# Layer 2's attention: the softmax division moved from the probabilities to a turned row that multiplies a head pair's outputs

## The chip, the core and the metric

The kernel runs as one program on one core of a Trainium2 chip. The metric is the device time of one execution in microseconds (us); the time before is the median of three runs. TensorE (PE in the profile) multiplies matrices, VectorE is DVE, ScalarE is ACT, GpSimd is POOL, SyncE (SP) issues most DMA transfers. Each engine takes its instructions in the order in which the program gives them and waits at semaphores for the others. TensorE writes PSUM banks; GpSimd works on SBUF.

## The reference, cut to what matters

Two layers over a sequence of 512 tokens and a width of 1024, batch 1, float32. The change lies in layer 2, which has two attentions over the same normed input: eight heads of a dilated window attention, and eight heads of a latent (low rank) attention.

```python
h = rmsnorm(x, norm_gain)
proj = jnp.matmul(h, w_in)
q_a, k_a, v_a, z_a, c_q, c_kv, k_rope, z_b = jnp.split(proj, idx, axis=-1)
...
# per head and block of 128 queries, in both attentions:
s = einsum(q, k) * scale + bias            # masked above the diagonal
p = exp(s - m)                             # m: row maximum
o = einsum(p, v) / sum(p)                  # the division this change moves
...
mixed = jnp.concatenate([o_a * jax.nn.silu(z_a), o_b * jax.nn.silu(z_b)], axis=-1)
out = x + jnp.matmul(mixed, w_out)
```

## The kernel before

All projections of both layers form a list of groups (`GROUPS`); a group is a product of 512 tokens by up to 512 columns, taken in up to 8 slabs of 128 rows of the weights, and a slab in four quarters `t`. Values are kept as a high and a low part, so a quarter is three matmuls of 512 columns (L1637 to L1639, tiles `w_hi`, `w_lo` with `hT_hi`, `hT_lo` or `cT_hi`, `cT_lo`). ACT makes `w_hi` of a slab (L564), POOL makes `w_lo` (L893), three slabs ahead of PE.

Layer 2's attentions have 16 heads in 8 pairs `p`: pairs 0 to 3 are of the dilated, 4 to 7 of the latent attention. A pair has four query blocks `i`, so there are `N` = 32 steps `n = 4p + i`, each with two heads `j`, and rows of 128(i+1) keys. The steps have no time of their own: a generator `heads()` on each engine is cut into three parts for each step (called a, b and c here), and `heads_due(v)` says how many parts are done by the time of projection quarter `v`, counted from the start of the group `G_VALUES`. On PE the parts stand between the projection matmuls of `G_VALUES`, the two `G_UKV` groups, `G_GATES` and the one after it, and the first half of `G_OUT2`, which is the first of the two groups of the final projection. On the other engines the same parts stand between the casts of weights, evacuations and the norms of the latent attention (`latent_norms`, rows L1100 to L1117 and L1548 to L1556 on DVE; `latent_queries` on POOL, L957 and L961).

What a step does before the change:

1. PE: scores of both heads into banks `A[0]` and `A[1]` (L1843).
2. DVE: adds bias or mask, writes the negated scores into `probs` (tile `sgd_sb`) and their minimum into `nmax` (L1424).
3. ACT: `exps`, exponential in place with the row sum in `rsum` (L758).
4. DVE: reciprocal of the two sums into `rinv` (L1443).
5. POOL: `scale`, probabilities by reciprocal and by 0.5 (L1001), once for each head.
6. PE: `turn_probs`, transposes of the 128x128 blocks into the one bank `A[2]` (L1852), which waits for the scaling, and for DVE to have emptied `A[2]`.
7. DVE: `turned_probs`, copies them out to `turned_place` (L1433, tiles `pT` or `sgd_sb`).
8. PE, once for each pair: `outputs`, values by turned probabilities (L1866) into `A[3]`, which then holds the pair's outputs with heads and features on the partitions and the 512 queries on the columns. The trace counts 40 matmul records for them.
9. ACT: `pair_raw` copies `A[3]` to `o_raw(p)` (L746). POOL: `gate` multiplies by the gate (L1008). ACT: `split` makes the high part (L753). POOL: `low` makes the low part (L1016), which is the stationary or moving operand of slab `p` of the final projection.

`heads_turn` (L1826) transposes queries and keys of the coming pair, into `A[2]` too (the second of all into `A[3]`), and ACT empties it (L738). The first two of them stand at slab 4 of `G_VALUES`. They wait for the norms of the keys on DVE (L1177).

`heads_due` before: the first part at quarter 20, 9 parts by quarter 32, then one a quarter, and two a quarter from quarter 120; 106 parts in all.

Of the kernel before, what the change touches and what calls it, by code (L numbers as in the profile page):

```python
# [20 lines left out]
ALU = mybir.AluOpType  # L21
# [104 lines left out]
HEAD_STEPS = 3 * (4 * H + 3) + 1  # L126
HEADS_FIRST, HEADS_SECOND, HEADS_THIRD = 20, 33, 120
# [6 lines left out]
def heads_due(v):  # L134

    if v < HEADS_FIRST:
        return 0
    if v < HEADS_SECOND:
        return 9 * (v - HEADS_FIRST + 1) // (HEADS_SECOND - HEADS_FIRST)
    if v < HEADS_THIRD:  # L140
        return 9 + (v - HEADS_SECOND + 1)
    return min(HEAD_STEPS, 9 + HEADS_THIRD - HEADS_SECOND + 2 * (v - HEADS_THIRD + 1))

# [41 lines left out]
GATE_STEP = {19: 0, 20: 1, 21: 2, 22: 3, 29: 4, 30: 5, 31: 6, 35: 7}  # L185
SPLIT_STEP = {20: 0, 21: 1, 22: 2, 28: 3, 30: 4, 31: 5, 32: 6, 35: 7}
# [45 lines left out]
def build(nc, a):  # L232
    with ExitStack() as ctx:
# [89 lines left out]
        h_inv, h_scaled, h_pt, h_pt_out, h_o = sem("h_inv"), sem("h_scaled"), sem("h_pt"), sem("h_pt_out"), sem("h_o")  # L323
# [144 lines left out]
        def _(sp):  # L468
# [82 lines left out]
        def _(act):  # L551
# [188 lines left out]
            def heads():  # L740
# [3 lines left out]
                def pair_raw(p):  # L744
                    act.wait_ge(h_o, p + 1 if p < H - 1 else H + 1)
                    act.copy(o_raw(p), A[3][:, :]).then_inc(pair_out, 1)  # L746

                def split(n):
                    if n in SPLIT_STEP:
                        p = SPLIT_STEP[n]  # L750
                        act.wait_ge(pair_gated, p + 1)
                        act.wait_ge(z_ready, 4 * G_GATES if p < 3 else 4 * G_OUT2)
                        act.copy(pair_split(p)[0], o_raw(p)).then_inc(pair_hi, 1)  # L753
# [7 lines left out]
                for n in range(N + 3):  # L761
                    if n >= 7 and n % 4 == 3:
                        pair_raw(n // 4 - 1)
                    if n < N:
                        exps(n, 0)
                        exps(n, 1)
                    yield
                    if turn_at(n):
                        heads_turned(*turn_at(n))
                    yield  # L770
                    split(n)
                    yield
                pair_raw(H - 1)
                split(N + 3)
# [103 lines left out]
        def _(pool):  # L878
# [113 lines left out]
            def heads():  # L992
# [17 lines left out]

                def low(n):
# [6 lines left out]
                for n in range(N + 3):  # L1018
                    low(n - 1)
                    if 1 <= n < N + 1:  # L1020
                        scale(n - 1, 0)
                    yield
                    if 1 <= n < N + 1:
                        scale(n - 1, 1)
                    yield
                    gate(n)
                    yield
                gate(N + 3)
                low(N + 3)
# [54 lines left out]
        def _(dve):  # L1084
# [322 lines left out]
            def heads():  # L1407
# [27 lines left out]

                scores(0, 0)
                scores(0, 1)
                for n in range(N + 3):
                    if 0 <= n - 2 < N:
                        turned_probs(n - 2, 0)  # L1440
                    if 1 <= n < N + 1:
                        dve.wait_ge(h_exp, 2 * n)
                        dve.reciprocal(rinv[:, n - 1, 0:2], rsum[:, n - 1, 0:2]).then_inc(h_inv, 1)  # L1443
                    yield
                    yield
                    if 0 <= n - 2 < N:
                        turned_probs(n - 2, 1)
                    if n + 1 < N:
                        scores(n + 1, 0)
                        scores(n + 1, 1)  # L1450
                    yield
                yield
# [179 lines left out]
        def _(pe):  # L1632
# [197 lines left out]
            def heads():  # L1830
# [24 lines left out]

                def outputs(p, blocks):

                    pe.wait_ge(h_pt_out, 2 * (4 * p + blocks[-1]) + 2)
                    if p == 0:
                        pe.wait_ge(z_by_act, act_evacs[G_VALUES + 1])  # L1860
                    elif blocks[0] == 0:
                        pe.wait_ge(pair_out, p)
# [8 lines left out]
                for n in range(N + 3):  # L1871
                    if 0 <= n - 2 < N:
                        turn_probs(n - 2, 0)
# [12 lines left out]
                    if 0 <= n - 2 < N:  # L1886
                        turn_probs(n - 2, 1)
                    p, c = divmod(n - 6, 4)
                    if c == 0 and 0 <= p < H - 1:
                        outputs(p, range(4))  # L1890
                    if n == N + 1:
                        outputs(H - 1, range(3))
                    if n == N + 2:
# [20 lines left out]
            def project(g):  # L1914
# [22 lines left out]
                for k in range(0 if g else 1, nk):  # L1937
# [13 lines left out]
                    if k == 4 and g == G_VALUES:  # L1951
# [99 lines left out]
```

## Time and profile before

| what | value |
|---|---|
| time, median of 3 runs | 940.93 us (940.06 to 941.17) |
| profiled execution, its own time | 940.87 us |
| its span | 939.1 us |
| PE busy | 915.1 us, 97% |
| POOL busy | 473.7 us, 50% |
| ACT busy | 396.1 us, 42% |
| DVE busy | 394.2 us, 42% |
| granted clock of PE, mean | 0.998 |

The attention steps of layer 2 lie between about 737 and 906 us of the span. In a timeline a row gives the start, the time from the first start to the last end, and the instructions merged in it; ends of matmuls are modelled, so on PE the distance between two starts tells more than the length of a row. A wait in square brackets is idle time ahead of a row and the instruction that ended it.

### The profile page before, as it was taken

The page shows a single profiled execution, that of the slowest core. Times are in us where ns is not written, and L with a number is a line of the kernel's source. Part 1 is how long each engine was busy: PE and PEld are TensorE (multiplying, and loading weights), DVE is VectorE, ACT ScalarE, POOL GpSimd, SP SyncE. Part 2 cuts the span into 40 slices and gives each one's busy share as a digit, 9 for nine tenths or more (in the row PEclk, how much of TensorE's full clock was granted, in tenths as well). Part 3 has the DMA queues.
Part 4 walks back from the last instruction along what each step waited for, and adds up shares of the span by engine and source line. Part 5 has one row for each costly group of instructions (what it writes and reads, how often), then busy time and mean ns, then how long its engine had stood idle before and what let it go on. Part 6 is the DMA issues. An engine that isn't in the chain of part 4 may idle for free. (4 is left out here: it accounts for less than half of the span.)

```text
span 939.1 us, 12624 instructions
## 1 busy us (share of the span) xinstructions
PE 915.1 (97%) x4640; PEld 725.3 (77%) x4640; DVE 394.2 (42%) x951; ACT 396.1 (42%) x873; POOL 473.7 (50%) x440
## 2 busy tenths in 40 slices
PE   9999999999999999999999999999999988999988
PEld 7877888887888877777777788788888655677767
DVE  4310139044114413567474434415429756544521
ACT  4533442334223344454554432325535663555521
POOL 5543436434546654655444334553447494465662
PEclk9999999999999999999999999999999999999999
DMA  8422211322322322122112242332523221111113
GB/s 306 147 91 76 82 45 46 112 68 89 112 90 90 106 87 77 49 87 68 55 58 68 63 162 68 108 101 77 151 68 107 68 90 46 33 36 46 46 46 112
DMA packets 41709, 80.77 MB, mean 86 GB/s; under 512 B 3328, under 2 KB 5120, under 8 KB 41648
## 3 DMA queue, kind: packets, MB, share of 16 engines
q1 hardware_dynamic: 41504, 79.95, 27.2%
q8 instruction: 37, 0.61, 0.3%
q14 instruction: 24, 0.20, 0.1%
q10 hardware_dynamic: 144, 0.02, 0.0%
HBM read 77.84 MB, written 2.12 MB: 85 GB/s over the span
## 5 line engine op out<-in xcount | busy, mean ns | idle before, releaser
L893 POOL TENSOR_TENSOR w_lo<-raw,w_hi 128x512 fp32r<-128x512 f32 (+1 forms) x262 | 343.5, 1319 | 387.0 <-ACT w_hi L564 385.9
L1637 PE MATMUL Z<-w_hi,hT_hi 128*128 128x512 f32 (+1 forms) x804 | 324.2, 403 | 4.0 <-POOL w_lo L893 2.7
L1639 PE MATMUL Z<-w_hi,hT_lo 128*128 128x512 f32 (+1 forms) x804 | 313.1, 389 | 0.0
L1638 PE MATMUL Z<-w_lo,hT_hi 128*128 128x512 f32 (+1 forms) x804 | 312.3, 388 | 0.0
L564 ACT CAST w_hi<-raw 128x512 fp32r<-128x512 f32 (+1 forms) x262 | 157.3, 614 | 247.8 <-PE Z L1639 224.0
L1637 PEld LDWEIGHTS Z<-w_hi,hT_hi 128*128 128x128 f32 x804 | 151.1, 188 | 45.8 <-issue 12.9
L1639 PEld LDWEIGHTS Z<-w_hi,hT_lo 128*128 128x128 f32 x804 | 150.9, 188 | 31.5
L1638 PEld LDWEIGHTS Z<-w_lo,hT_hi 128*128 128x128 f32 x804 | 151.4, 188 | 26.8 <-issue 0.2
L1001 POOL TENSOR_SCALAR sgd_sb<-sgd_sb,rinv 128x128 f32<-128x128 f32 (+3 forms) x64 | 37.1, 587 | 42.9 <-DVE rinv L1443 42.1
L1637 PE MATMUL Z<-w_hi,oT_hi 128*128 128x512 f32 x128 | 51.1, 399 | 0.5 <-DVE prob L1209 0.5
L1358 DVE CUSTOM_DVE_ANT_0 x_sb<-A,bias 128x128 f32<-128x128 f32 (+3 forms) x64 | 28.6, 484 | 53.8 <-PE A L1766 53.8
L717 ACT ACTIVATE x_sb<-x_sb,nmax 128x128 f32<-128x128 f32 (+3 forms) x64 | 35.4, 555 | 36.4 <-DVE nmax L1358 36.4
L1639 PE MATMUL Z<-w_hi,oT_lo 128*128 128x512 f32 x128 | 50.0, 391 | 0.0
L1638 PE MATMUL Z<-w_lo,oT_hi 128*128 128x512 f32 x128 | 49.9, 390 | 0.0
L758 ACT ACTIVATE sgd_sb<-sgd_sb,nmax 128x128 f32<-128x128 f32 (+3 forms) x64 | 35.5, 556 | 30.1 <-DVE nmax L1424 30.1
L1433 DVE COPY pT<-A 128x384 f32<-128x384 f32 (+2 forms) x40 | 22.3, 556 | 42.3 <-PE A L1852 39.9
L1852 PE MATMUL A<-ident,sgd_sb 128*128 128x128 f32 x160 | 29.9, 286 | 8.4 <-POOL sgd_sb L1001 4.0
L1852 PEld LDWEIGHTS A<-ident,sgd_sb 128*128 128x128 f32 x160 | 19.2, 142 | 23.6 <-DVE pT L1433 8.2
L1843 PE MATMUL A<-kT,qT 64*128 64x128 f32 (+7 forms) x128 | 34.2, 454 | 0.1
L1235 DVE TENSOR_TENSOR x_sb<-x_sb,Z 128x512 f32<-128x512 f32 x16 | 10.9, 688 | 52.8 <-PE Z L1639 52.8
L1637 PE MATMUL Z<-hT_hi,w_hi 128*128 128x512 f32 x64 | 32.3, 505 | 0.0
L580 ACT ACTIVATE z_sb<-Z,rms 128x512 f32<-128x512 f32 (+1 forms) x40 | 26.2, 682 | 12.7 <-PE Z L1639 12.5
(220 smaller groups left out, 1204.1 us busy)
## 6 DMA issues: line engine op xcount, KB each, us to landing
raw<-in_w_in SPq DMA_DIRECT2D x91, 512.0 KB, 3.6
raw<-in_w_out SPq DMA_DIRECT2D x16, 512.0 KB, 3.4
x_sb<-in_x SPq DMA_DIRECT2D x8, 512.0 KB, 5.6
raw<-in_ret_w_o SPq DMA_DIRECT2D x8, 512.0 KB, 3.3
raw<-in_diff_w_o SPq DMA_DIRECT2D x8, 512.0 KB, 3.4
out<-x_sb SPq DMA_DIRECT2D x8, 256.0 KB, 2.8
raw<-in_w_in SPq DMA_DIRECT2D x4, 416.0 KB, 3.2
sgd_sb<-in_xT SPq DMA_DIRECT2D x3, 512.0 KB, 7.1
```

The costliest lines, as they stand in the source:

```text
L564: act.copy(w_hi[:, s % SPLIT_SLOTS, 0:width], raw[:, c % RAW_SLOTS, s - CHUNK_START[c], 0:width]).then_inc(hi_ready, 1)
L580: act.activation((z_ret if g < G_RET else z_sb)[:, t, arg:arg + width], Z[t][:, 0:width], ACT.Copy, scale=rms[:, layer, 0, t:t + 1]).then_ ...
L717: act.activation(p, p, ACT.Exp, bias=nmax[:, j, n:n + 1], scale=-1.0, accum_out=rsum[:, n, j:j + 1]).then_inc(s_exp, 1)
L758: act.activation(probs[:, n % 4, j, 0:w], probs[:, n % 4, j, 0:w], ACT.Exp, bias=nmax[:, j, n:n + 1], scale=-1.0, accum_out=rsum[:, n, j:j ...
L893: pool.tensor_tensor(w_lo[:, s % SPLIT_SLOTS, 0:width], raw[:, c % RAW_SLOTS, s - CHUNK_START[c], 0:width], w_hi[:, s % SPLIT_SLOTS, 0:wid ...
L1001: pool.tensor_scalar(p, p, rinv[:, n, j:j + 1], 0.5, ALU.mult, ALU.mult).then_inc(h_scaled, 1)
L1358: dve.tensor_tensor_reduce(diff_probs(j, n, w), A[j][:, score_columns(i, True)], bias[:, h % 2, S - w:S], -1.0, TOP, ALU.add, ALU.min, nma ...
L1637: pe.matmul(out, l_hi, r_hi, start=first, stop=False)
L1638: pe.matmul(out, l_hi, r_lo, start=False, stop=False)
L1639: return pe.matmul(out, l_lo, r_hi, start=False, stop=last)
L1843: pe.matmul(A[j][:, score_columns(i, shared)], qT[rows, slot, P * i:P * (i + 1)], kT[rows, slot, 0:P * (i + 1)], start=True, stop=True).th ...
L1852: last = pe.transpose(A[2][:, kk], probs[:, m % 4, j, kk], ident[:, :])
```

## The change

What it does:

- `scale` on POOL is gone. `turn_probs` waits for the exponentials, and transposes unscaled probabilities.
- The reciprocals of a pair (8 columns) are taken by one DVE instruction at the pair's last step, in place of four of 2 columns.
- `pair_spread` (ACT) spreads them over 512 columns into `o_raw(p)`. `turn_row` (PE) transposes the four 128x128 blocks of this into `row_bank(p)`, which is `A[3]` (for the last pair `A[0]`). `pair_row` (ACT) copies the bank back to `o_raw(p)`.
- `outputs` waits for that copy, since it writes the same bank. `pair_end` (DVE) then multiplies the bank, 0.5 and the row. It stands in the place of ACT's `pair_raw`. For the last pair POOL multiplies the row by the gate beforehand (`row_gated`), and ACT's high part follows `pair_end` at once.
- The parts of a step stand in another order, and the first pair's `heads_turn` stands one slab later (slab 5). `heads_due` starts at quarter 23 with one part a quarter to the end; 103 parts in all. The bias of pair 2 is loaded two slabs earlier in SP's queue.

```diff
-HEAD_STEPS = 3 * (4 * H + 3) + 1
-HEADS_FIRST, HEADS_SECOND, HEADS_THIRD = 20, 33, 120
+HEAD_STEPS = 3 * (4 * H + 2) + 1
+HEADS_FIRST = 23
...
-    return min(HEAD_STEPS, 9 + HEADS_THIRD - HEADS_SECOND + 2 * (v - HEADS_THIRD + 1))
+    return max(0, min(HEAD_STEPS, v - HEADS_FIRST + 1))
...
+        def row_bank(p):
+            return A[3] if p < H - 1 else A[0]
...
-                for p, at in enumerate(((G_LAYER2 + 1, 0), (G_LAYER2 + 1, 0), (G_GATES, 6), (G_GATES + 1, 0))):
+                for p, at in enumerate(((G_LAYER2 + 1, 0), (G_LAYER2 + 1, 0), (G_GATES, 4), (G_GATES + 1, 0))):
...  ACT
-                def pair_raw(p):
-                    act.wait_ge(h_o, p + 1 if p < H - 1 else H + 1)
-                    act.copy(o_raw(p), A[3][:, :]).then_inc(pair_out, 1)
+                def pair_spread(p):
+                    act.wait_ge(h_inv, p + 1)
+                    r = rinv[:, 4 * p:4 * p + 4, :].rearrange("p i j -> p (i j)").unsqueeze(2).broadcast_to([P, 8, 64])
+                    act.copy(o_raw(p).rearrange("p (n e) -> p n e", e=64), r).then_inc(row_spread, 1)
+
+                def pair_row(p):
+                    act.wait_ge(row_turned, p + 1)
+                    act.copy(o_raw(p), row_bank(p)[:, :]).then_inc(row_evicted, 1)
...
-                if g == G_VALUES and k == 4:
+                if g == G_VALUES and k == 5:
                     heads_turned(0, 0)
                     heads_turned(0, 1)
...  POOL
-                def scale(n, j):
-                    w = P * (n % 4 + 1)
-                    if j == 0:
-                        pool.wait_ge(h_inv, n + 1)
-                    p = probs[:, n % 4, j, 0:w]
-                    pool.tensor_scalar(p, p, rinv[:, n, j:j + 1], 0.5, ALU.mult, ALU.mult).then_inc(h_scaled, 1)
...
+                def row_gated(p):
+                    pool.wait_ge(row_evicted, p + 1)
+                    pool.wait_ge(th_used, 8 + p + 1)
+                    pool.tensor_tensor(o_raw(p), o_raw(p), gateT[:, p, :], ALU.mult).then_inc(pair_first, 1)
...  DVE
+                def pair_end(p):
+                    if p == H - 1:
+                        dve.wait_ge(pair_first, 1)
+                    dve.wait_ge(h_o, p + 1 if p < H - 1 else H + 1)
+                    dve.scalar_tensor_tensor(o_raw(p), A[3][:, :], 0.5, o_raw(p), ALU.mult, ALU.mult).then_inc(pair_out, 1)
...
+                    if n < N and n % 4 == 3:
+                        dve.wait_ge(h_exp, 2 * n + 2)
+                        dve.reciprocal(rinv[:, n - 3:n + 1, :], rsum[:, n - 3:n + 1, :]).then_inc(h_inv, 1)
...  PE
-                    pe.wait_ge(h_scaled, 2 * m + j + 1)
+                    pe.wait_ge(h_exp, 2 * m + j + 1)
...
+                def turn_row(p):
+                    pe.wait_ge(row_spread, p + 1)
+                    if p == H - 1:
+                        pe.wait_ge(h_max, 8 * H)
+                    elif p:
+                        pe.wait_ge(pair_out, p)
+                    for i in range(4):
+                        cc = slice(P * i, P * (i + 1))
+                        last = pe.transpose(row_bank(p)[:, cc], o_raw(p)[:, cc], ident[:, :])
+                    last.then_inc(row_turned, 1)
```

Where the instructions stand now. First PE, between the last two pairs, in the order before. The projection matmuls between the rows are left out; L1852 turns probabilities, L1843 are scores, L1866 a pair's outputs.

```order
L1852 MATMUL A<-ident,sgd_sb 128x128 [waits h_scaled,h_pt_out]
L1852 MATMUL A<-ident,sgd_sb 128x128 x3
...
L1843 MATMUL A<-kT,qT 128x384 [waits h_max] x2
...
L1852 MATMUL A<-ident,sgd_sb 128x128 [waits h_scaled,h_pt_out]
L1852 MATMUL A<-ident,sgd_sb 128x128 x3
...
L1852 MATMUL A<-ident,sgd_sb 128x128 [waits h_scaled,h_pt_out]
...
L1843 MATMUL A<-kT,qT 128x512 [waits h_max] x2
...
L1852 MATMUL A<-ident,sgd_sb 128x128 [waits h_scaled,h_pt_out]
L1866 MATMUL A<-sgd_sb,m_sb 64x128 [waits pair_out,h_pt_out]
```

The same place on PE now, where L1865 turns probabilities, L1879 turns the row, L1856 are scores and L1894 the outputs.

```order
L1865 MATMUL A<-ident,sgd_sb 128x128 [waits h_exp,h_pt_out]
L1865 MATMUL A<-ident,sgd_sb 128x128 x3
L1879 MATMUL A<-ident,z_sb 128x128 [waits pair_out,row_spread]
L1879 MATMUL A<-ident,z_sb 128x128 x3
...
L1865 MATMUL A<-ident,sgd_sb 128x128 [waits h_exp,h_pt_out]
L1865 MATMUL A<-ident,sgd_sb 128x128 x3
...
L1856 MATMUL A<-kT,qT 128x384 [waits h_max] x2
...
L1894 MATMUL A<-sgd_sb,m_sb 64x128 [waits row_evicted,h_pt_out]
L1894 MATMUL A<-sgd_sb,m_sb 64x128 x5
L1894 MATMUL A<-pT,m_sb 64x128 x14
L1865 MATMUL A<-ident,sgd_sb 128x128 [waits h_exp,h_pt_out]
```

The outputs moved ahead of the next pair's first turn and of the widest scores, and the row's turn stands behind the first four-block turn; the wait for scaling became one for exponentials.

Second, PE at the end of the attention, before: the two four-block turns and the last pair's outputs, with hardly a projection between.

```order
L1852 MATMUL A<-ident,sgd_sb 128x128 [waits h_scaled,h_pt_out]
L1852 MATMUL A<-ident,sgd_sb 128x128 x2
L1852 MATMUL A<-ident,sgd_sb 128x128 [waits h_scaled,h_pt_out]
L1852 MATMUL A<-ident,sgd_sb 128x128 x3
...
L1852 MATMUL A<-ident,sgd_sb 128x128 [waits h_scaled,h_pt_out]
L1852 MATMUL A<-ident,sgd_sb 128x128 x3
L1866 MATMUL A<-pT,m_sb 64x128 [waits pair_out,h_pt_out]
```

And the same place now.

```order
L1865 MATMUL A<-ident,sgd_sb 128x128 [waits h_exp,h_pt_out]
L1865 MATMUL A<-ident,sgd_sb 128x128 x3
L1879 MATMUL A<-ident,z_sb 128x128 [waits h_max,row_spread]
L1879 MATMUL A<-ident,z_sb 128x128 x3
L1894 MATMUL A<-pT,m_sb 64x128 [waits pair_out,h_pt_out]
L1894 MATMUL A<-pT,m_sb 64x128
L1894 MATMUL A<-sgd_sb,m_sb 64x128 x4
L1894 MATMUL A<-pT,m_sb 64x128 x6
...
L1865 MATMUL A<-ident,sgd_sb 128x128 [waits h_exp,h_pt_out]
L1865 MATMUL A<-ident,sgd_sb 128x128 x3
```

Three of four output blocks moved ahead of the last turn, and none of the rows waits for scaling.

Third, DVE between the last two pairs. L1433 before and L1436 now empty the turned probabilities, L1424 and L1427 write the masked scores, L1443 is before the reciprocal and now `pair_end`. Before:

```order
L1433 COPY pT<-A2 128x128 [waits h_o,h_pt]
L1443 RECIPROCAL rinv<-rsum 128x2 [waits h_exp]
L1433 COPY pT<-A2 128x128 [waits h_o,h_pt]
L1424 ISA sgd_sb,nmax<-A0,dist 128x512 [waits h_mm,h_pt]
L1424 ISA nmax 128x1
L1424 ISA sgd_sb,nmax<-A1,dist 128x512 [waits h_mm,h_pt]
L1424 ISA nmax 128x1
L1433 COPY sgd_sb<-A2 128x256 [waits h_o,h_pt]
L1443 RECIPROCAL rinv<-rsum 128x2 [waits h_exp]
```

Now:

```order
L1436 COPY pT<-A2 128x128 [waits h_o,h_pt]
L1443 SCALAR_TENSOR_TENSOR z_sb<-A3,z_sb 128x512 [waits h_o]
L1427 ISA sgd_sb,nmax<-A0,dist 128x512 [waits h_mm,h_pt]
L1427 ISA nmax 128x1
L1436 COPY sgd_sb<-A2 128x256 [waits h_o,h_pt]
L1427 ISA sgd_sb,nmax<-A1,dist 128x512 [waits h_mm,h_pt]
L1427 ISA nmax 128x1
L1436 COPY sgd_sb<-A2 128x256 [waits h_o,h_pt]
```

The two scores of a step no longer stand side by side ahead of a copy, the reciprocals with their wait for the exponentials are gone from three steps in four, and a 512 column product is new.

## Rows read from the trace of the kernel before

**Rows 1.** Page, part 1: busy time, share of the span, instructions.
```profile
PE 915.1 (97%) x4640; PEld 725.3 (77%) x4640; DVE 394.2 (42%) x951; ACT 396.1 (42%) x873; POOL 473.7 (50%) x440
```

**Rows 2.** Windows: length, busy time by engine, PE clock, DMA share and rate.
```profile
800.00:840.00 40.00, 39.54 (x259) 28.08 (x257) 19.78 (x64) 21.40 (x53) 19.71 (x25) 1.00 0.14 41
...
900.00:902.00 2.00, 2.00 (x11) 1.40 (x12) 0.79 (x2) 0.00 (x0) 0.62 (x1) 0.50 0.04 9
```

**Rows 3.** Waits of PE, 720 to 939 us: total us, times, longest.
```profile
PE A L1852 <- POOL sgd_sb L1001: 4.0, 2, 2.4
PE A L1852 <- DVE sgd_sb L1433: 2.2, 1, 2.2
PE A L1826 <- DVE z_sb L1177: 1.4, 1, 1.4
PE A L1826 <- DVE sgd_sb L1433: 1.2, 2, 0.7
PE A L1852 <- DVE pT L1433: 1.2, 1, 1.2
PE A L1826 <- DVE pT L1433: 0.7, 1, 0.7
```

**Rows 4.** Timeline of PE, a quiet stretch of pairs 6 and 7.
```profile
883.52 0.39 PE L1638 MATMUL Z<-w_lo,cT_hi 128*128 128x512 f32 x1
883.75 0.40 PE L1639 MATMUL Z<-w_hi,cT_lo 128*128 128x512 f32 x1
883.99 0.60 PE L1852 MATMUL A<-ident,sgd_sb 128*128 128x128 f32 x4
884.34 0.47 PE L1637 MATMUL Z<-w_hi,cT_hi 128*128 128x512 f32 x1
...
884.88 0.40 PE L1639 MATMUL Z<-w_hi,cT_lo 128*128 128x512 f32 x1
885.37 0.33 PE L1852 MATMUL A<-ident,sgd_sb 128*128 128x128 f32 x1
...
888.61 0.39 PE L1639 MATMUL Z<-w_hi,hT_lo 128*128 128x512 f32 x1
888.84 0.27 PE L1852 MATMUL A<-ident,sgd_sb 128*128 128x128 f32 x1
889.05 0.88 PE L1866 MATMUL A<-sgd_sb,m_sb 128*64 128x128 f32 x12
889.75 1.70 PE L1866 MATMUL A<-pT,m_sb 128*64 128x128 f32 x28
891.38 0.50 PE L1637 MATMUL Z<-w_hi,hT_hi 128*128 128x512 f32 x1
```

**Rows 5.** Timeline of PE, end of the attention.
```profile
895.54 0.40 PE L1639 MATMUL Z<-w_hi,hT_lo 128*128 128x512 f32 x1
895.89 0.55 PE L1852 MATMUL A<-ident,sgd_sb 128*128 128x128 f32 x3
898.86 0.63 PE L1852 MATMUL A<-ident,sgd_sb 128*128 128x128 f32 x4 [2.42 <-POOL sgd_sb L1001]
...
900.27 1.12 PE L1852 MATMUL A<-ident,sgd_sb 128*128 128x128 f32 x4
...
906.35 0.50 PE L1637 MATMUL Z<-w_hi,hT_hi 128*128 128x512 f32 x1
```

**Rows 6.** Timeline of POOL and ACT, end of the attention.
```profile
898.02 1.36 POOL L1001 TENSOR_SCALAR sgd_sb<-sgd_sb,rinv 128x512 f32<-128x512 f32 x2
...
906.46 0.58 ACT L746 COPY z_sb<-A 128x512 f32<-128x512 f32 x1 [1.06 <-PE A L1866]
```

**Rows 7.** Timelines of DVE and of POOL around 773 us.
```profile
773.27 0.18 DVE L1100 TENSOR_SCALAR rs_b<-rs_a 128x32 int32<-128x32 int32 x1
...
773.97 1.23 DVE L1103 TENSOR_TENSOR rs_b<-rstd 128x32 f32<-128x32 f32 x1
...
773.87 1.29 POOL L961 TENSOR_TENSOR z_sb<-z_sb,o_sb 128x512 f32<-128x512 f32 x1
```

More of the change, by code:

```diff
@@ L322, in build @@
         h_turned, h_qk, h_mm, h_max, h_exp = sem("h_turned"), sem("h_qk"), sem("h_mm"), sem("h_max"), sem("h_exp")
-        h_inv, h_scaled, h_pt, h_pt_out, h_o = sem("h_inv"), sem("h_scaled"), sem("h_pt"), sem("h_pt_out"), sem("h_o")
+        h_inv, h_pt, h_pt_out, h_o = sem("h_inv"), sem("h_pt"), sem("h_pt_out"), sem("h_o")
+        row_spread, row_turned, row_evicted, pair_first = (sem(n) for n in ("row_spread", "row_turned", "row_evicted", "pair_first"))
         w_first, x_hi, x_lo = sem("w_first"), sem("x_hi"), sem("x_lo")
@@ L759, in exps @@
                                    scale=-1.0, accum_out=rsum[:, n, j:j + 1]).then_inc(h_exp, 1)
-                for n in range(N + 3):
-                    if n >= 7 and n % 4 == 3:
-                        pair_raw(n // 4 - 1)
+                for n in range(N + 2):
+                    if n >= 5 and n % 4 == 1 and n < N:
+                        pair_row(n // 4 - 1)
                     if n < N:
@@ L766, in heads @@
                         exps(n, 1)
+                    if n >= 4 and n % 4 == 0:
+                        pair_spread(n // 4 - 1)
                     yield
@@ L770, in heads @@
                     yield
+                    if n == N:
+                        pair_row(H - 1)
                     split(n)
                     yield
-                pair_raw(H - 1)
-                split(N + 3)
+                split(N + 2)
                 yield
@@ L1016, in low @@
                         pool.tensor_tensor(lo_, o_raw(p), hi_, ALU.subtract).then_inc(pair_lo, 1)
-                for n in range(N + 3):
+                for n in range(N + 2):
                     low(n - 1)
-                    if 1 <= n < N + 1:
-                        scale(n - 1, 0)
+                    if n == N + 1:
+                        row_gated(H - 1)
                     yield
-                    if 1 <= n < N + 1:
-                        scale(n - 1, 1)
                     yield
@@ L1027, in heads @@
                     yield
-                gate(N + 3)
-                low(N + 3)
+                low(N + 2)
                 yield
@@ L1434, in turned_probs @@
                                     A[2][:, 0:P * (i + 1)].rearrange("p (b s) -> p b s", s=P)).then_inc(h_pt_out, 1)
+                def pair_end(p):
[3 more added lines that the diff above has]
+                    dve.scalar_tensor_tensor(o_raw(p), A[3][:, :], 0.5, o_raw(p), ALU.mult, ALU.mult).then_inc(pair_out, 1)
                 scores(0, 0)
                 scores(0, 1)
[L1438 to L1445, printed above, removed]
+                for n in range(N + 2):
                     if 0 <= n - 2 < N:
                         turned_probs(n - 2, 1)
+                    if n >= 6 and n % 4 == 2 and n < N:
+                        pair_end((n - 6) // 4)
+                    yield
                     if n + 1 < N:
                         scores(n + 1, 0)
+                    yield
+                    if 1 <= n < N + 1:
+                        turned_probs(n - 1, 0)
+                    if n + 1 < N:
                         scores(n + 1, 1)
+                    if n < N and n % 4 == 3:
+                        dve.wait_ge(h_exp, 2 * n + 2)
+                        dve.reciprocal(rinv[:, n - 3:n + 1, :], rsum[:, n - 3:n + 1, :]).then_inc(h_inv, 1)
                     yield
+                pair_end(H - 1)
                 yield
@@ L1860, in outputs @@
                         pe.wait_ge(z_by_act, act_evacs[G_VALUES + 1])
+                    if p < H - 1:
+                        pe.wait_ge(row_evicted, p + 1)
                     elif blocks[0] == 0:
@@ L1870, in heads @@
                 scores(0, (0, 1))
-                for n in range(N + 3):
+                for n in range(N + 2):
                     if 0 <= n - 2 < N:
-                        turn_probs(n - 2, 0)
+                        turn_probs(n - 2, 1)
                     yield
@@ L1885, in heads @@
                     yield
-                    if 0 <= n - 2 < N:
-                        turn_probs(n - 2, 1)
-                    p, c = divmod(n - 6, 4)
+                    p, c = divmod(n - 5, 4)
                     if c == 0 and 0 <= p < H - 1:
                         outputs(p, range(4))
+                    if 1 <= n < N + 1:
+                        turn_probs(n - 1, 0)
+                    if n >= 4 and n % 4 == 0:
+                        turn_row(n // 4 - 1)
+                    if n == N:
+                        outputs(H - 1, range(3))
                     if n == N + 1:
-                        outputs(H - 1, range(3))
-                    if n == N + 2:
                         outputs(H - 1, (3,))
```

17 lines of the change are left out of this document (7 added, 10 removed).

## The prediction

> **What bounds the kernel now.** I read the page's busy shares first: PE is busy 97% of the span and no other engine over 50% [rows 1]. So the time is PE's own work plus PE's idle time, and anything on another engine counts only where PE waits for it. Then the windows: in 800 to 840 us, in the middle of layer 2's attention, PE is busy 39.54 of 40 us at a granted clock of 1.00, its level of 2.4 GHz [rows 2]. There the change can win nearly nothing and can only add PE work. Then PE's waits from 720 us on, which is where the change lies [rows 3]. They are 10.7 us in all, and every one ends at a transposition. They have three kinds: waits for POOL's scaling (two, together 4.0 us, the longest 2.4 at the end of the attention [rows 5]), one of 1.4 us for the norms of the keys ahead of the very first turn, and five for DVE to have emptied bank A[2] (2.2 + 1.2 + 1.2 + 0.7, together 5.3 us). Last the timeline, since ends of matmuls are modelled and distances between starts are safer. Projection matmuls follow each other at 0.23 us (883.52 to 883.75) [rows 4], so whatever a distance has over that is the work or the wait between.
>
> **The change, part by part.** The sum is made against the profiled execution's own 940.87 us (span 939.1, the rest around it), which is 0.06 under the median of 940.93.
>
> *The turned row, added PE work.* Eight pairs get four transpositions each, L1879. Four of the same shape cost 884.34 - 883.75 - 0.23 = 0.36 us between two projection matmuls, and the next matmul starts some 0.08 late as well: 0.44 us [rows 4]. Lower bound 0.36, since in front of them stand other transpositions for all pairs, so no change of kind is paid twice; upper bound the whole merged row, 0.60. I take 0.44, eight times: **+3.5 us** (2.9 to 4.8). None of it can be hidden on a full PE.
>
> A page speaks against this price. The Trainium skill, "TensorE: Matmul & The Clock Gate", Part 4 (PE-mode transpose), gives about 275 ns for a 128x128 transposition in a kernel's context. A lone one here does read 0.27 us (at 888.84) [rows 4], so the trace agrees for one by itself, but four of them need 0.44 together. By the page's figure taken 32 times the term would be an estimated 8.8 us in place of 3.5; by the rows it is 3.5.
>
> *Scaling leaves POOL.* 64 instructions go. What that gives PE is the two waits, of which 1.6 us lie near 759 us and the 2.4 us belong to the end, below: **-1.6 us**. What comes next there is the exponential on ACT, which stands five or six parts ahead of the turn, so nearly five quarters of about 0.69 us (three matmuls), more than an exponential's row with its hops; I book nothing for it.
>
> *The end of the attention.* From the projection matmul at 895.54 to that at 906.35 there are 10.81 us [rows 5]. In it lie ten starts of projection matmuls, 2.3 us. The other 8.5 us are a three-block and two four-block turns and the last pair's 40 output matmuls. At quiet prices: a pair's outputs and one transposition take 891.38 - 888.61 - 0.23 = 2.54 us [rows 4], two gaps of four 0.88, one of three some 0.35, and 0.1 for splitting the outputs: 3.9 us. So 4.6 us are wait, and its echo. PE stood 2.42 us for POOL, whose scaling began only at 898.02 [rows 6], behind other work in its queue. After that the granted clock was 0.50 in 900 to 902, which is the level of 1.2 GHz [rows 2], and the four-block turn took 1.12 us against 0.63 at 898.86 [rows 5]. In the new order nothing in this stretch waits for POOL, one part stands in each quarter, the exponentials of the last step are some five parts old, and three of four output blocks need only turns that lie behind. **-4.6 us** (2.4 if the slow clock and the short waits came all the same). Behind it the chain to the last slab shrinks: `pair_end` on DVE (bounded by ACT's copy of this size, 0.58 [rows 6], and twice that), the high part, the low part, against eight quarters or 5.5 us of projections. It lies hidden. It would cost if POOL were over 2 us late there.
>
> *The first turn, one slab later.* Four quarters, 2.8 us, stand ahead of it now, and the wait was 1.4: **-1.4 us**, with what is late next (DVE's norms) below.
>
> *The five waits for A[2].* Here the order on DVE decides. Before, both scores of a step stood together between two copies; now there is one score between copies. Reciprocals with their wait for ACT fall from 32 to 8. Against that `pair_end` is new, 8 times some 0.6 to 0.7 us, in a part with one copy. The largest waits are in 765 to 790 us, where DVE also has the latent norms to do, and these run slow: a 128x32 instruction takes 1.23 us at 773.97 while one of the same width took 0.18 just before, and it ends when a POOL instruction ends that began at 773.87 and took 1.29 [rows 7]. The POOL work that stays (rotations and low parts) still does that, but the scaling no longer does, and no longer delays the rotations. I take half of the 5.3 us: **-2.6 us** (0 to -5.3). The value is in the middle since rows speak for both.
>
> The page "SBUF — State Buffer" of the Trainium skill, section "SBUF: two separate sides", says that VectorE and GpSimd share one port pair as an exclusive lock, held for a whole instruction. The trace agrees [rows 7]. By that rule less POOL work is worth more than its own waits.
>
> *Short waits of the old order.* The one-block turn behind a four-block turn waits for the copy: 885.37 - 884.88 - 0.23 = 0.26 us [rows 4], in seven pairs, 1.8 us. In the new order the row's turn or the outputs stand between. Three four-block turns behind a `heads_turn` of the first pairs wait about as much. Of 2.6 us I take **-2.2** (0 to -2.6).
>
> *New waits.* `turn_row` waits for `pair_spread`: one ACT instruction of 512 columns (0.58 by the nearest row [rows 6]) behind two exponentials and a reciprocal. From the turn that releases the last DVE score to the row's turn PE has three quarters, 2.1 us, and two turns, 0.8; the chain needs some 2.3. `outputs` waits for `pair_row`, again 0.58, across two quarters. ACT gains 8 copies of 0.58, in the first pairs where it is nearly full. I book **+0.6** (0 to 3; behind the waiting PE all projections queue). Other edits (the bias load two slabs earlier in SP's queue, which waits for scores that are long done) cost nothing; if the load held up a weight transfer, it has 12 quarters of cover.
>
> Sum: 3.5 - 1.6 - 4.6 - 1.4 - 2.6 - 2.2 + 0.6 = -8.3 us. 940.87 - 8.3 = **932.6 us**.
>
> **The rivals.**
> *DVE bounds the first half.* PE gets to the early turns sooner, but the norms on DVE end no sooner, and the waits that are removed there come back as waits for A[2]. Then 1.6, 1.4 and 2.6 fall out: -8.3 + 5.6 = -2.7, **938.2 us**. For it: the waits for A[2] are already the larger part and rows 7 show DVE held up by POOL work that stays. Against it: after these 50 us DVE has room.
> *DVE is freed wholly.* The other 2.7 of the 5.3 go too and there is no new wait: **929.3 us**.
> *Transpositions don't overlap.* If each of the 32 new ones cost its own 0.27 us, as the single one does [rows 4], they are 8.6 us, 5.1 more than booked: **937.7 us**. The four-block rows speak against it. The page on TensorE named above would have it so.
> *The row comes late (slower).* In each pair reciprocal, spread, turn, copy and outputs form a chain across ACT. If the spread with its repeated elements is slow, or ACT is behind, PE stands in part c of each pair with all projections behind it. The slack is about 0.5 us; with 8.3 us gained elsewhere it decides from 1.0 us of wait a pair. A spread of four times 0.58 us would be 1.7 late, 1.2 of wait; with ACT's later work pushed back, and a clock that falls as at 900 us, I take 1.5 a pair: 12 us, less the 0.6 booked: **944 us**. For it speaks only that the operation isn't in the trace.
>
> **How the numbers follow.** Forecast 0.60, DVE bound 0.15, DVE freed 0.13, no overlap 0.04, late row 0.08. A measurement of this kernel can tell about 0.2%, 1.9 us, from no change. The first four cases are faster by more than that, though the DVE bound case with a row some 0.2 us late a pair is within: faster 0.88, same 0.05, slower 0.07. The range takes in the freed case and its best prices at the lower end (929.3 less some of the 0.6 that the row's lower bound gives), and most of the DVE bound case at the upper: 928.5 to 937.5. Left out are the late row and what of the second case lies above.
>
> **What would show it.** In the changed kernel's profile: no POOL instruction on `sgd_sb` in the attention; at its end the four-block turns without an idle time ahead, and a clock of 1.00 there; the row's turns with a distance of 0.4 to 0.5 us over the projections and little idle ahead; ACT's spread at about 0.6 us; PE's waits for copies from A[2] down to about 3 us, all before 790 us. PE busy time should be up by some 2 to 3 us where the records count the new turns. The forecast is wrong if PE waits for `row_spread` or `row_evicted` in every pair, if the early waits come back whole, or if the clock falls at some new place.

## The result and the profile after

The changed kernel takes 930.32 us (median of 4 runs, 929.72 to 930.96) against 940.92 us for the kernel before (4 runs, 940.06 to 941.17). The ratio is 0.9889, with a 95% interval from 0.9872 to 0.9906: 10.6 us or 1.1% faster. The profiled execution took 930.71 us, its span is 928.9 us against 939.1. One later execution of the changed kernel ran at a granted clock of 0.75 and took 1134.08 us; it is left out where its repeat is compared below.

The page, part 1, of the changed kernel (busy time, share of the span, instructions) answers to [rows 1]:

```profile
PE 913.7 (98%) x4672; PEld 728.1 (78%) x4672; DVE 396.3 (43%) x935; ACT 400.6 (43%) x881; POOL 438.3 (47%) x376
```

The 32 new transpositions are there (4672 against 4640) and POOL lost 64 instructions and 35 us. PE is still the bound. Its busy time did not rise. Ends of matmuls are modelled longer than their distance, so that waits up to some 0.15 us (a row reads 0.39 us where the next starts after 0.23) count as busy, and so do slow matmuls at half the clock; both became fewer. A busy sum is no price for an added instruction here, the distances between starts are.

The waits of PE from 715 us on (total us, times, longest), against [rows 3]:

```profile
PE A L1865 <- DVE pT L1436: 1.6, 2, 0.8
PE A L1839 <- DVE sgd_sb L1436: 1.1, 1, 1.1
PE Z L1650 <- POOL w_lo L901: 0.2, 1, 0.2
PE A L1839 <- DVE pT L1436: 0.2, 1, 0.2
```

No wait for scaling is left, none for the norms of the keys ahead of the first turn, and none for `row_spread` or `row_evicted`. The waits for DVE to empty `A[2]` fell from 5.3 to 2.9 us.

The end of the attention on PE (start, time, instructions), against [rows 5]:

```profile
887.84 0.40 PE L1652 MATMUL Z<-w_hi,hT_lo 128*128 128x512 f32 x1
888.19 0.55 PE L1865 MATMUL A<-ident,sgd_sb 128*128 128x128 f32 x3
...
889.97 0.60 PE L1865 MATMUL A<-ident,sgd_sb 128*128 128x128 f32 x4
890.40 0.60 PE L1879 MATMUL A<-ident,z_sb 128*128 128x128 f32 x4
890.93 0.44 PE L1894 MATMUL A<-pT,m_sb 128*64 128x128 f32 x4
...
893.21 0.60 PE L1865 MATMUL A<-ident,sgd_sb 128*128 128x128 f32 x4
...
895.13 1.09 PE L1894 MATMUL A<-pT,m_sb 128*64 128x128 f32 x16
896.15 0.50 PE L1650 MATMUL Z<-w_hi,hT_hi 128*128 128x512 f32 x1
```

From 887.84 to 896.15 there are 8.31 us with 16 projection starts of 0.2275 (four took 0.91 us from 729.62 to 730.53 in the kernel before), so 4.7 us are left for the same turns and outputs and the row's turn. Before, it was 8.5 us without the row. The clock stayed up, as the windows show (length, busy by engine, clock, DMA share, GB/s), where [rows 2] had 0.50:

```profile
888.00:892.00 4.00, 4.00 (x39) 3.33 (x39) 1.49 (x4) 2.10 (x4) 3.70 (x3) 1.00 0.02 4
892.00:896.00 4.00, 4.00 (x39) 3.08 (x34) 0.69 (x1) 0.76 (x2) 3.24 (x3) 1.00 0.42 131
```

The price of the row, in a quiet pair of the changed kernel:

```profile
813.90 0.40 PE L1652 MATMUL Z<-hT_hi,w_lo 128*128 128x512 f32 x1
814.13 0.60 PE L1865 MATMUL A<-ident,sgd_sb 128*128 128x128 f32 x4
814.57 0.60 PE L1879 MATMUL A<-ident,z_sb 128*128 128x128 f32 x4
814.92 0.47 PE L1650 MATMUL Z<-hT_hi,w_hi 128*128 128x512 f32 x1
```

Eight transpositions take 814.92 - 813.90 - 0.23 = 0.79 us, four took 0.36 in [rows 4]: the row costs 0.43 us a pair. Yet a quiet pair did not get longer. From one pair's outputs to the next the kernel before takes 870.94 - 850.98 = 19.96 us, the changed one 859.09 - 839.22 = 19.87:

```profile
850.98 0.88 PE L1866 MATMUL A<-sgd_sb,m_sb 128*64 128x128 f32 x12
...
870.94 0.44 PE L1866 MATMUL A<-pT,m_sb 128*64 128x128 f32 x4
```

```profile
839.22 0.88 PE L1894 MATMUL A<-sgd_sb,m_sb 128*64 128x128 f32 x12
...
859.09 0.44 PE L1894 MATMUL A<-pT,m_sb 128*64 128x128 f32 x4
```

The first fence is of the kernel before, the second of the changed one. So some 0.5 us of short waits went in each such pair, of which most are too short to be listed as waits. The largest of them is the second one-block turn: it stood 0.26 us late in [rows 4], and now PE starts it at once:

```profile
842.19 0.40 PE L1652 MATMUL Z<-hT_hi,w_lo 128*128 128x512 f32 x1
842.42 0.27 PE L1865 MATMUL A<-ident,sgd_sb 128*128 128x128 f32 x1
842.45 0.48 PE L1650 MATMUL Z<-hT_hi,w_hi 128*128 128x512 f32 x1
```

Over the projections it costs 842.45 - 842.19 - 0.23 = 0.03 us, where the same turn cost 0.33 before (at 866.83).

What the new instructions of the other engines cost (ACT and DVE groups from 740 us on: count, busy us, mean ns, idle before and releaser):

```profile
L744 ACT COPY z_sb<-rinv 128x512 f32<-128x512 f32 x5 | 3.0, 605 | 1.0 <-DVE rinv L1462 1.0
L748 ACT COPY z_sb<-A 128x512 f32<-128x512 f32 x5 | 2.9, 587 | 5.7 <-PE A L1879 5.7
L1443 DVE SCALAR_TENSOR_TENSOR z_sb<-A,z_sb 128x512 f32<-128x512 f32 x5 | 3.4, 683 | 1.8 <-PE A L1894 1.8
```

Reading one element 64 times costs ACT hardly more than the copy of the row out of PSUM: 605 ns against 587. `pair_end` took 683 ns, in the 0.6 to 0.7 us that the prediction gave it.

### The profile page after: what moved, and what is told of

It reads as the page before. It is cut to its first block, busy times and chain, and to the rows that moved or that the text cites. A ratio compares the mean times of both kernels' runs of the same rounds, so it can differ in the third digit from the quotient of the medians.

```text
span 928.9 us, 12622 instructions
## 1 busy us (share of the span) xinstructions
PE 913.7 (98%) x4672; PEld 728.1 (78%) x4672; DVE 396.3 (43%) x935; ACT 400.6 (43%) x881; POOL 438.3 (47%) x376
## 4 chain that ended last, share of the span: by engine, by line
PE 88%; DVE 5%; POOL 2%; issue 2%; ACT 1%; DMA 1%; SPq 0%; ACTq 0%; DVEq 0%; POOLq 0%
PE Z L1650 24%; PE Z L1652 23%; PE Z L1651 23%; PE A L1856 3%; PE A L1779 2%; PE A L1894 2%; PE A L1865 2%; PE A L1791 2%; PE A L1660 2%; POOL w_lo L901 1%; PE A L1839 1%; PE A L1804 1%; PE Z L1737 1%; PE A L1690 1%; PE A L1764 1%
## 5 line engine op out<-in xcount | busy, mean ns | idle before, releaser
L1436 DVE COPY pT<-A 128x384 f32<-128x384 f32 (+2 forms) x40 | 22.3, 557 | 34.6 <-PE A L1865 34.4
L1856 PE MATMUL A<-kT,qT 64*128 64x128 f32 (+7 forms) x128 | 33.8, 451 | 0.0
L1865 PEld LDWEIGHTS A<-ident,sgd_sb 128*128 128x128 f32 x160 | 19.1, 140 | 16.0 <-DVE pT L1436 5.9
L1865 PE MATMUL A<-ident,sgd_sb 128*128 128x128 f32 x160 | 29.5, 282 | 2.0 <-DVE pT L1436 1.6
L1162 DVE TENSOR_REDUCE stat<-bias 128x4 f32<-128x512 f32 (+1 forms) x16 | 10.7, 683 | 42.8 <-POOL bias L913 42.8
```

Of the source, the lines that this page charges most:

```text
L1436: dve.tensor_copy(turned_place(m, j), A[2][:, 0:P * (i + 1)].rearrange("p (b s) -> p b s", s=P)).then_inc(h_pt_out, 1)
L1856: pe.matmul(A[j][:, score_columns(i, shared)], qT[rows, slot, P * i:P * (i + 1)], kT[rows, slot, 0:P * (i + 1)], start=True, stop=True).th ...
L1865: last = pe.transpose(A[2][:, kk], probs[:, m % 4, j, kk], ident[:, :])
```

## The experiments

My theory was that of the prediction: PE gained the waits, POOL's share of them through the dependency, the others through the order on DVE, and paid 0.43 us a pair. The rivals were that the order alone, or the algebra alone, or POOL's mere occupancy made the gain.

**The algebra alone**, in the old order of steps, with the old end (two parts a quarter) and the first turn at slab 4. Cut from the difference to the kernel before:

```diff
-                    pe.wait_ge(h_scaled, 2 * m + j + 1)
+                    pe.wait_ge(h_exp, 2 * m + j + 1)
...  PE, part a, behind turn_probs(n - 2, 0)
+                    if n >= 5 and n % 4 == 1:
+                        turn_row(n // 4 - 1)
```

> The turned row in the old order of steps: turns wait for exponentials, the row's turn stands behind the first four-block turn's partner, outputs where they were, two parts a quarter at the end, first turn at slab 4. Theory A: before's 940.9 + 3.4 for the row's turns - 1.7 for the scaling wait near 759 us - 3.7 for the wait and the slow clock at the end = 938.9 us (937.5 to 940). Rival (the order brings nothing): 930 to 932 us. Other rival (the algebra brings nothing): 944 us.

Measured: 936.68 us (median of 7 runs), ratio 0.9961 (0.9949 to 0.9974), beside 940.6 us for the kernel before. A little better than my 938.9, under its lower bound: the waits for `A[2]` fell as well, from 5.3 to 3.3 us, with no change on DVE but the missing reciprocals and `pair_end`.

```profile
PE A L1869 <- DVE pT L1441: 1.7, 3, 0.7
PE A L1843 <- DVE z_sb L1185: 1.4, 1, 1.4
PE A L1843 <- DVE sgd_sb L1441: 0.9, 2, 0.7
PE A L1843 <- DVE pT L1441: 0.7, 1, 0.7
```

These are PE's waits in it. Those for scaling are gone, also at the old, packed end. From the projection start at 894.26 to the one at 902.03, with ten projection starts, 5.5 us are left for the same turns and outputs, the row's turn among them, where it was 8.5.

**The order alone**, with scaling on POOL kept and no row; the first turn one slab later and one part a quarter at the end belong to it. Cut from the difference to the changed kernel:

```diff
-                    pe.wait_ge(h_exp, 2 * m + j + 1)
+                    pe.wait_ge(h_scaled, 2 * m + j + 1)
...
-                    if n >= 4 and n % 4 == 0:
-                        turn_row(n // 4 - 1)
...  ACT, part a
+                    if n >= 6 and n % 4 == 2 and n < N:
+                        pair_raw((n - 6) // 4)
```

> The new order of steps alone: probabilities are scaled on GpSimd as before, no turned row, ScalarE copies the outputs, one reciprocal a step. Theory A (the wait for GpSimd was a cause of its own): the row's 3.4 us are saved, but waits for the scaling return, 1.6 us or more around 755 us and 2 to 4 us at the end: 931 to 934 us. Rival (the order is all of the gain): 930.3 - 3.4 = 926.9 us, and no wait for GpSimd above 0.5 us.

Measured: 938.07 us (7 runs), ratio 0.9973 (0.9959 to 0.9986). Slower than either forecast, though it has no row to turn. PE's waits:

```profile
PE A L1849 <- POOL sgd_sb L1005: 5.5, 6, 1.7
PE A L1849 <- DVE pT L1429: 2.6, 4, 0.9
PE A L1823 <- DVE sgd_sb L1429: 1.1, 1, 1.1
```

The new order takes up the turn of head 0 one part earlier. With scaling in the chain that makes PE wait for POOL six times in place of two: 4.7 of the 5.5 us are four waits between 752 and 781 us. At the end it is otherwise:

```profile
894.48 0.40 PE L1636 MATMUL Z<-w_hi,hT_lo 128*128 128x512 f32 x1
895.47 0.52 PE L1849 MATMUL A<-ident,sgd_sb 128*128 128x128 f32 x3 [0.59 <-POOL sgd_sb L1005]
...
903.50 0.50 PE L1634 MATMUL Z<-w_hi,hT_hi 128*128 128x512 f32 x1
```

In these 9.02 us lie 16 projection starts, so 5.4 us are left for the turns and outputs, and the clock is 1.00 in 892 to 904 us. So either half alone takes some 3 of the 3.9 us that the end gained (8.54 to 4.67). The sum comes out otherwise because of the early pairs: alone the two halves bring 2.5 and 3.9 us, together 10.3 (against 940.6), that is 3.8 us more than their sum.

**POOL kept busy.** The changed kernel, with POOL doing 64 multiplications of the old sizes (for the last pair one block less in the widest) at the old places on dead columns, for which no other engine waits:

```diff
+                    if 1 <= n < N + 1:
+                        idle_scale(n - 1, 0)
...
+                    pool.tensor_scalar(spare, dead, cols[:, 41:42], 0.5, ALU.mult, ALU.mult).then_inc(idle_done, 1)
```

> The changed kernel (930.3 us), with GpSimd still doing as many multiplications of the same sizes at the places of the old scaling, but on dead columns of z_sb, and nobody waits for them. Theory A (TensorE gained because its turns no longer wait for GpSimd): within 1 us of 930.3, TensorE's waits for copies out of A[2] stay near the 2.9 us of the changed kernel. Rival B (GpSimd's occupancy was what held up VectorE, by blocked instructions and later rotations): 932.3 us or more, waits for A[2] back to about 5 us.

Measured: 933.34 us (4 runs), ratio 0.9925 (0.9909 to 0.9941). Against the 930.3 of the changed kernel 3.0 us are back, and rival B is right: PE's waits for `A[2]` are 5.6 us (with one of 0.2 that isn't shown), against 2.9 in the changed kernel and 5.3 before.

```profile
PE A L1880 <- DVE pT L1451: 4.3, 4, 2.7
PE A L1854 <- DVE sgd_sb L1451: 1.1, 1, 1.1
```

The 2.7 us stand ahead of the turn at 777.83, and where they come from stands on DVE and POOL in this run. The rows are of both engines in order of time:

```profile
773.86 0.68 POOL L1013 TENSOR_SCALAR z_sb<-z_sb,cols 128x512 f32<-128x512 f32 x1
773.96 0.62 DVE L1122 SCALAR_TENSOR_TENSOR rs_b<-rs_b,rs_a 128x32 f32<-128x32 f32 x1
774.51 1.26 POOL L902 TENSOR_TENSOR w_lo<-raw,w_hi 128x512 fp32r<-128x512 f32 x1
774.61 1.21 DVE L1123 SCALAR_TENSOR_TENSOR rstd<-rs_b,rstd 128x32 f32<-128x32 f32 x1
...
776.52 0.19 DVE L1122 SCALAR_TENSOR_TENSOR rs_b<-rs_b,rs_a 128x32 f32<-128x32 f32 x1
```

A DVE instruction of 32 columns takes 0.19 us by itself at 776.52. When it starts behind a POOL instruction it ends with that one: 0.62 and 1.21 us. Five DVE instructions are held so between 770 and 776 us. Two of them, the shortest held (0.46 and 0.62 us), lie under added multiplications; two lie under rotations (L970) and one under a low part (L902), which the added work had pushed back to these places. The cost is confined to this stretch: one pair takes 23.02 us from outputs to outputs in place of 20.32, the quiet pairs 19.86 as in the changed kernel (19.87). The Trainium skill, "SBUF — State Buffer", section "SBUF: two separate sides", has the two engines share one port pair as an exclusive lock; the rows agree.

**The end, packed as before**: the changed kernel with two parts a quarter from quarter 120.

```diff
+    if v < HEADS_THIRD:
+        return max(0, v - HEADS_FIRST + 1)
+    return min(HEAD_STEPS, HEADS_THIRD - HEADS_FIRST + 2 * (v - HEADS_THIRD + 1))
```

> The changed kernel with two parts of a step a quarter from quarter 120 on, as before the change. Theory A (the end gained by the scaling that left its chain): 930.3 to 931 us. Rival (it gained because its parts are spread over more projection quarters): 932.5 to 934 us, with TensorE's waits for VectorE's copies or for the row at the end.

Measured: 930.66 us (4 runs), ratio 0.9893 (0.9878 to 0.9908). The difference of 0.3 us is within the scatter of the runs, so no gain from the wider spacing is shown. The end gained without it, as the two halves above did.

**The first turn back at slab 4:**

```diff
-                if g == G_VALUES and k == 5:
+                if g == G_VALUES and k == 4:
                     heads_turned(0, 0)
...  PE
-                    if k == 5 and g == G_VALUES:
+                    if k == 4 and g == G_VALUES:
```

> The changed kernel with the first pair's turn of queries and keys back at slab 4 of its group. Theory A (it gained the wait for the norms): 930.3 + 1.6 = 931.9 us, an idle time of 1.4 us ahead of that turn. Rival (VectorE bounds the first pairs, so the later start is made up there): 930.3 us, with the 1.4 us taken out of later waits for A[2].

Measured: 931.62 us (4 runs), ratio 0.9900 (0.9885 to 0.9915), 1.3 us over the changed kernel. Its waits are

```profile
PE A L1865 <- DVE pT L1436: 1.6, 2, 0.9
PE A L1839 <- DVE z_sb L1180: 1.4, 1, 1.4
PE A L1839 <- DVE sgd_sb L1436: 1.1, 1, 1.1
```

The wait is back and the later ones are as they were, so nothing was made up.

**The row turned twice:**

```diff
-                    for i in range(4):
+                    for i in (0, 1, 2, 3, 0, 1, 2, 3):
```

> The changed kernel with each pair's row turned twice into the same bank: 32 transpositions more. Theory A (four take 0.43 us behind other transpositions): 930.3 + 3.4 = 933.7 us. Rival (each costs its own 0.27 us): 930.3 + 8.6 = 938.9 us. If a late row were hidden so far, more than 3.4.

Measured: 933.08 us (4 runs), ratio 0.9915 (0.9901 to 0.9930): +2.8 us for 32 transpositions, 0.35 a pair. In a quiet pair the second four add 0.44: 816.65 - 815.19 - 0.23 = 1.23 us in place of 0.79.

```profile
815.19 0.39 PE L1652 MATMUL Z<-hT_hi,w_lo 128*128 128x512 f32 x1
815.42 0.60 PE L1865 MATMUL A<-ident,sgd_sb 128*128 128x128 f32 x4
815.85 1.04 PE L1879 MATMUL A<-ident,z_sb 128*128 128x128 f32 x8
816.65 0.48 PE L1650 MATMUL Z<-hT_hi,w_hi 128*128 128x512 f32 x1
```

Some of it was time in which PE would have waited: the waits for `pT` fell from 1.6 to 1.2 us. At 0.27 us each they would have cost 8.6 us; that rival is refuted.

**No turn of the row.** The reciprocals are spread but not turned, and the outputs are multiplied by the unturned row; so the kernel leaves out the division by the sums in its right form.

```diff
-                    act.copy(o_raw(p).rearrange("p (n e) -> p n e", e=64), r).then_inc(row_spread, 1)
+                    act.copy(o_raw(p).rearrange("p (n e) -> p n e", e=64), r).then_inc(row_evicted, 1)
...
-                    if n >= 5 and n % 4 == 1 and n < N:
-                        pair_row(n // 4 - 1)
...
-                    if n >= 4 and n % 4 == 0:
-                        turn_row(n // 4 - 1)
```

> The changed kernel without the turn of the row and ScalarE's copy of it: the spread reciprocals multiply the outputs unturned, so the softmax division is left out of the computation in its right form. Theory A (the row costs TensorE its instructions only): 930.3 - 3.4 = 926.9 us. Rival (its waits or ScalarE's copies delay others too): 925 us or less.

Measured: 929.33 us (4 runs), ratio 0.9874 (0.9860 to 0.9889). Taking the whole turn away brings 1.0 us, not 3.4. Both forecasts were wrong, and the timeline of PE tells why:

```profile
813.72 0.60 PE L1861 MATMUL A<-ident,sgd_sb 128*128 128x128 f32 x4
814.08 0.48 PE L1646 MATMUL Z<-hT_hi,w_hi 128*128 128x512 f32 x1
...
814.63 0.40 PE L1648 MATMUL Z<-hT_hi,w_lo 128*128 128x512 f32 x1
815.11 0.66 PE L1861 MATMUL A<-ident,sgd_sb 128*128 128x128 f32 x4
815.52 0.47 PE L1646 MATMUL Z<-hT_hi,w_hi 128*128 128x512 f32 x1
```

The second four-block turn now starts 815.11 - 814.63 - 0.23 = 0.25 us late, since DVE's copy out of `A[2]` (L1432) stands from 814.36 to 815.05. In the changed kernel the row's turn, which uses another bank, stands between the two and fills that time. In the first pairs a larger wait takes its place (PE's waits for `pT` are 2.7 us in this run, 1.6 in the changed kernel). So most of the row's cost is covered.

It is covered by its place. From outputs to outputs the same quiet pair takes 19.87 us in the changed kernel and 19.73 without the turn (838.55 to 858.28): 0.14 us for the row. In the old order the second four-block turn had no such wait, and there the row costs its whole price: 20.42 us in the run with the algebra alone (848.69 to 869.11) against 19.96 before.

**Less for DVE.** The changed kernel, with the last part of the latent keys' norm (four products and four copies) moved to POOL, which now has gaps of 5 us there:

```diff
+            def latent_keys(step):
+                t = step // 2
+                k4 = z_sb[:, :, Z_KCAT:Z_KCAT + 768].rearrange("p t (h e) -> p t h e", h=H)
+                kv4 = m_sb[:, :, :].rearrange("p t (h e) -> p t h e", h=H)
+                if step == 0:
+                    pool.wait_ge(k_rstd, 1)
+                if step % 2 == 0:
+                    last = pool.tensor_tensor(k4[:, t, :, 0:NOPE], kv4[:, t, :, 0:NOPE],
+                                              rstd[:, 64 + 8 * t:72 + 8 * t].unsqueeze(2).broadcast_to([P, H, NOPE]), ALU.mult)
+                else:
+                    last = pool.tensor_scalar(k4[:, t, :, NOPE:MLA_K],
+                                              k_rope[:, t, :].unsqueeze(1).broadcast_to([P, H, ROPE]), 1.0, 1.0,
+                                              ALU.mult, ALU.mult)
+                last.then_inc(k_latent, 1)
```

> The changed kernel with the last part of the latent keys' norm (four products of 512 columns and four copies) moved from VectorE to GpSimd, which has gaps of 5 us there now. Theory A (what is left of the waits for A[2] is VectorE's load and blocking): the 1.1 us wait near 789 us goes and some of the 0.8 near 776, 928.5 to 929.3 us. Rival (GpSimd's longer instructions block VectorE and the low parts instead): 931 us or more.

Measured: 929.09 us (4 runs), ratio 0.9873 (0.9856 to 0.9889). The 1.1 us wait near 789 us is gone, the two others stayed. I ran it again beside the changed kernel and a third one on one chip:

> The kernel whose last part of the key norm runs on GpSimd, once more: 929.1 us, 1.2 us under the changed kernel on the same chip.

> The changed kernel unaltered, beside the next two on one chip: 930.3 us.

Measured: 928.61 us (4 runs, 928.06 to 928.70), and for the changed kernel 930.21 to 931.38 us in three runs. So the gain, 2.0 us here, is beyond the scatter.

The third is the kernel just measured, with the Newton steps of this norm at quarters 46 and 49, two each, in place of 45 to 48, and POOL's parts one quarter later:

```diff
-LATENT_PIECES = (23, 25, 27, 29, 31, *range(45, 50))
+LATENT_PIECES = (23, 25, 27, 29, 31, 46, 46, 49, 49, 50)
-KEY_PARTS = {50 + i: i for i in range(8)}
+KEY_PARTS = {51 + i: i for i in range(8)}
```

> The same, with VectorE's Newton steps for the key norm moved from four quarters in a row to two that follow a part c, after which TensorE's next turn doesn't need VectorE at once. Theory A (the waits of 0.8 and 0.85 us near 772 and 776 come from VectorE being held just ahead of a copy of part c): both go, 927.5 to 928 us. Rival (VectorE simply has too much to do there): the waits move, 929 us.

Measured: 927.37 us (4 runs), ratio 0.9866 (0.9849 to 0.9882). Its only wait of PE from 715 us on is

```profile
PE Z L1664 <- POOL w_lo L903: 0.2, 1, 0.2
```

All waits for `A[2]` that were long enough to be listed are gone. The one near 789 us went when DVE had less to do; the two of 0.8 us went with the same work at other times, so these two were not forced by its amount. At 3 us under the changed kernel and 13 under the one before it is the fastest of this study.

## Why the prediction was right

The forecast was 932.6 us, the range 928.5 to 937.5, and the time 930.3. The range held it; the gain was 10.6 us where 8.3 were summed. By the terms:

| term | booked | measured in the trace |
|---|---|---|
| the row's turns | +3.5 | +3.4 (8 x 0.43), by the run without them 1.0 |
| scaling wait near 759 us | -1.6 | -1.6, gone |
| end of the attention | -4.6 | -4.3 (8.5 to 4.7 less 0.4 for the row) |
| first turn a slab later | -1.4 | -1.6 between starts; 1.3 by the run |
| waits for `A[2]` | -2.6 | -2.4 (5.3 to 2.9) |
| short waits | -2.2 | about -3.7, as what is left |
| new waits | +0.6 | 0 |
| sum | -8.3 | -10.2 (spans 939.1 and 928.9) |

**The row.** The price from the four-block turn held to 0.1 us. The step "None of it can be hidden on a full PE" failed: the row stands where PE would wait for the bank, so that its removal gives 1.0 us and not 3.4. I had named such a cover ("the row's turn or the outputs stand between"), but only for the one-block turn. This term and the short waits are tied. They can be divided as in the table, or as +1.0 and about -1.3; either way the two together were booked at +1.3 and came to -0.3.

**The short waits** are the term that was mis-sized, by 1.5 us. I priced the waits of the 0.26 us kind in seven pairs and three more. The quiet pair shows 0.5 us, from places of which I had named only the first. Over the projections, the second one-block turn costs 0.03 us in place of 0.33, the first four-block turn 0.36 in place of 0.53 (the row's share taken off), and the widest scores 1.77 in place of 1.95. Against that the second three-block turn costs 0.42 in place of 0.25, a short new wait. The number of places at which PE leaves the projections is 12 in both, so fewer late starts are not the reason.

**The new waits** for the row did not come. The spread took 0.61 us, where ACT's copy took 0.59, so that "the row comes late" had no base. No wait for `row_spread` or `row_evicted` is listed in any pair.

**Waits for `A[2]`.** The half that I took was the right size, but it was a middle between two readings, and that it fitted is partly luck: "Here the order on DVE decides" is not what the runs show. With POOL busy the waits are 5.6 us in the new order, no better than before; in the old order with POOL free and fewer reciprocals they are 3.3. So POOL's occupancy made most of the difference, not the order of copies and scores. (The order alone with the scaling has 4.1 us of them, but there PE also waits 5.5 us for POOL and gets to the bank later.) Of the rival "DVE bounds the first half" only one term comes back with POOL as busy as before: that run took 933.3 us and not 938.2, since what the first turn and the scaling gave stayed. The upper end of the range, 937.5, lay below that rival's 938.2, so the range did not hold that case's own time, though the prediction says that it takes in most of it.

**The end.** The term held: the wait for POOL and the slow clock behind it are gone. The runs show two ways to get there, the scaling out of the chain in the old order (8.5 to 5.5 us with the row) or the new order with the scaling (8.5 to 5.4 without it). "One part stands in each quarter" was not needed; packed as before the changed end loses nothing that can be told from scatter.

**Signs named.** No scaling, clock 1.00 at the end, 0.43 us for a row, spread at 0.6 us, and waits down to about 3 us before 790: seen. That PE's busy time should be up by some 2 to 3 us was wrong, it fell by 1.4.

What stays open: the 3.7 us of short waits are a remainder, checked in quiet pairs alone. The order of steps was not taken apart further, so that each place's share in them outside these pairs isn't known.

## What to carry to other kernels

On an engine that is 97% busy, price an edit by distances between starts on either side of it, and ask what the new work covers: a turn into another bank just ahead of one that waits for its own bank cost a third of its price, and its whole price where nothing waited behind it. Work taken off an engine that holds up its neighbour can gain through the neighbour too: here 3 of 10 us came back when POOL did the same work for nobody, all in the stretch where DVE was short of time. A new order and a shorter chain can each bring little alone and still overlap in one place, as at the end here; test both halves before one is credited.

## What the runs showed of the hardware

- A DVE instruction of 128x32 took 0.19 us alone, and 1.21 us when it began 0.1 us behind a POOL subtraction of 128x512 that took 1.26.
- ACT spreading 8 columns to 512 (each read 64 times) takes 605 ns, a copy of 128x512 from PSUM 587 ns.
- Transpositions of 128x128 in float32 that follow each other into one bank cost 0.11 us each between projections (0.43 and 0.44 for four more). One alone reads 0.27 us, yet between two projection starts it adds 0.03, and the start behind it is 0.08 late.
- At the old end PE stood 2.42 us and then ran at a granted clock of 0.50 (900 to 902 us); in the changed kernel, without that wait, it stayed at 1.00 (888 to 896 us), and so it did with the order alone, where the longest wait for POOL at the end was 0.59 us (892 to 904 us).
